# Four experts of 32 slots side by side in TensorE's array, in place of pairs of 64

## The reference

```python
g = jnp.argmax(g_logits, axis=-1)                 # one of 4 groups
top_v, top_e = lax.top_k(e_logits, 2)             # two of its 8 experts
weight = p_group * jax.nn.softmax(top_v, axis=-1)
# the 512 (token, expert) entries are sorted by expert, and for every expert e:
hid = jax.nn.silu(xc @ w_gate[e]) * (xc @ w_up[e])    # 1024 -> 256, twice
out = hid @ w_down[e]                                  # 256 -> 1024
# each token adds its two outputs, times their weights
```

## Time and profile before

| | us |
|---|---|
| median of 3 runs | 2312.27 (2310.9 to 2316.02) |
| the profiled execution | 2313.08, its span 2311.3 |
| weights of the experts start to load | 216.5 |
| first and last expert matmul | 253.3, 488.8 |
| PE busy over the span | 1864.6 (81%) |

### The profile page before, as it was taken

How to read it: one execution, slowest core, us unless ns; L and a number is a source line. 1 busy time by engine, 2 the same in 40 slices (tenths; PEclk the granted TensorE clock), 3 DMA queues, 4 the chain that set the end, 5 groups by cost and what they waited for, 6 DMA issues and landing times. The chain is left out here.

```text
span 2311.3 us, 20289 instructions
## 1 busy us (share of the span) xinstructions
PE 1864.6 (81%) x6462; PEld 993.5 (43%) x6462; DVE 1307.9 (57%) x3163; ACT 612.0 (26%) x1396; POOL 741.8 (32%) x707
## 2 busy tenths in 40 slices
PE   5887899959877988786778788988789787776877
PEld 3556322329555444332333336756444433332333
DVE  4455300037277556667676646545756666667664
ACT  3353111123622222222222214543222222222221
POOL 1000154310103443453534420330443344453542
PEclk9998899979988899898988998998899999898999
DMA  8843999967548999999999977543999999999997
GB/s 291 318 165 143 375 400 399 401 207 232 208 160 314 409 410 409 421 422 421 421 422 410 422 321 248 183 163 102 342 409 409 412 421 422 421 421 421 413 422 293
DMA packets 211846, 786.03 MB, mean 340 GB/s; under 512 B 29243, under 2 KB 89403, under 8 KB 145948
## 3 DMA queue, kind: packets, MB, share of 16 engines
q0 software_dynamic: 85408, 547.20, 57.7%
q1 hardware_dynamic: 126332, 237.53, 28.5%
HBM read 806.56 MB, written 13.98 MB: 355 GB/s over the span
## 5 line engine op out<-in xcount | busy, mean ns | idle before, releaser
L1845 PE MATMUL psum<-peer_rows,peer_diag 128*128 128x512 f32 x2048 | 978.3, 638 | 271.0 <-ACT peer_diag L1901 270.9
L1938 POOL DMA_INDIRECT peer_rows<-in_peer_uv,peer_expert x512 | 580.0, 1133 | 882.1 <-PE psum L1845 673.6
L2017 DVE CUSTOM_DVE_ANT_0 peer_rows<-peer_rows,peer_norm_h 128x1024 f32<-128x1024 f32 x512 | 620.0, 1224 | 429.3 <-DMA peer_rows<-in_peer_uv,peer_expert 429.2
L1845 PEld LDWEIGHTS psum<-peer_rows,peer_diag 128*128 128x128 f32 x2048 | 412.3, 205 | 821.0 <-issue 502.6
L1901 ACT ACTIVATE peer_diag<-ident,peer_weight 128x128 f32<-128x128 f32 x512 | 164.8, 390 | 739.3 <-DVE peer_weight L2027 703.7
L1217 PE MATMUL psum<-moe_ring,moe_W 128*64 128x512 f32 x640 | 145.4, 600 | 16.2 <-DMA moe_ring<-in_moe_w,moe_piece_i 9.7
L1824 PE MATMUL psum<-peer_norm_hT,peer_q_raw 128*128 128x256 f32 x512 | 118.4, 387 | 9.8 <-DMA peer_q_raw<-in_peer_q 6.6
L1824 PEld LDWEIGHTS psum<-peer_norm_hT,peer_q_raw 128*128 128x128 f32 x512 | 98.2, 194 | 33.8 <-DMA peer_q_raw<-in_peer_q 11.4
L1293 POOL COPY moe_W<-moe_X 128x512 f32 x40 | 24.3, 620 | 252.5 <-issue 196.7
L1217 PEld LDWEIGHTS psum<-moe_ring,moe_W 128*64 128x64 f32 x640 | 46.8, 138 | 111.3 <-issue 111.1
L1894 ACT ACTIVATE peer_dots<-peer_dots 128x4 f32<-128x4 f32 (+1 forms) x140 | 28.5, 204 | 248.4 <-DVE peer_dots L2017 248.2
(11 more groups left out here) (425 smaller groups left out, 2245.0 us busy)
## 6 DMA issues: line engine op xcount, KB each, us to landing
moe_ring<-in_moe_w SPq DMA_DIRECT2D x192, 512.0 KB
mix_mod_w<-in_mod_w SPq DMA_DIRECT2D x32, 768.0 KB, 7.1
peer_q_raw<-in_peer_q SPq DMA_DIRECT2D x32, 512.0 KB
fox_w_raw<-in_fox_in SPq DMA_DIRECT2D x32, 512.0 KB
mix_w_raw<-in_w_in SPq DMA_DIRECT2D x24, 512.0 KB
lru_mod_w<-in_mod_w SPq DMA_DIRECT2D x16, 768.0 KB
fox_mod_w<-in_mod_w SPq DMA_DIRECT2D x16, 768.0 KB, 6.8
lru_in_raw<-in_lru_in SPq DMA_DIRECT2D x22, 512.0 KB
```

What stands on the lines that cost most here:

```text
L1845: ins = pe.matmul(Y(t, c), diag[:, j % 2, k, :], R[:, place_of(m), D + c * BANK:D + (c + 1) * BANK], start=m % PICKS == 0, stop=m % PICKS ...
L1938: pool.indirect_dma_start(R[:, place_of(m), :], None, uv, bass.IndirectOffsetOnAxis(ap=expert[:, t, at:at + 1], axis=0))\
L2017: dve.tensor_tensor_reduce(here, here, norm.h[:, t, :], 1.0, 0.0, ALU.mult, ALU.add, dots[:, t, at:at + 1]).then_inc(dotted, 1)
```

## The change

A group is now four subs of 32 slots (`BY = 4`, `SUB = 32`). The experts make eight own groups. Four overflow groups follow own groups 2, 3, 5 and 6: they hold 16 subs, for experts with more than 32 tokens (each up to 8 subs in all). Four experts use 32 columns each of the array. The ring keeps its 30 places, and a group now has 24 pieces. POOL makes four cuts a group, and 24 requests an overflow group. The table on which partition belongs to which sub is made by comparisons with multiples of 32 (`block_of`), and the tables of overflow subs have 16 rows in place of 8.

```diff
-    SUB = P // 2
-    OVER = 8
-    EXTRA = 3
+    BY = 4
+    SUB = P // BY
+    OVER = 16
+    EXTRA = 7
     SUBS = EXPERTS + OVER
-    PAIRS = SUBS // 2
+    QUADS = SUBS // BY
...
-    order = []
-    for p in range(EXPERTS // 2):
-        order.append(p)
-        if p % 3 == 0 and 0 < p < 13:
-            order.append(EXPERTS // 2 + p // 3 - 1)
-    is_extra = lambda x: order[x] >= EXPERTS // 2
+    own = EXPERTS // BY
+    order = [0, 1, 2, own, 3, own + 1, 4, 5, own + 2, 6, own + 3, 7]
+    is_extra = lambda x: order[x] >= own
...
-            turn += [(x, j, a) for j in range(GP) for a in range(2)]
+            turn += [(x, j, a) for j in range(GP) for a in range(BY)]
...
-                    sp.dma_start(ring[:, q % LAND, :], d["moe_w"][(2 * order[x] + a) * PIECES + j]).then_inc(landed[q % LAND], 16)
+                    sp.dma_start(ring[:, q % LAND, :], d["moe_w"][(BY * order[x] + a) * PIECES + j]).then_inc(landed[q % LAND], 16)
...
                 def gate_up(x):
-                    pe.wait_ge(cut, 2 * x + 2)
+                    pe.wait_ge(cut, BY * x + BY)
                     wait_past(pe, hid_done, x)
                     for j in range(GP):
-                        pair = [number_of[x, j, a] for a in range(2)]
-                        for q in pair:
+                        four = [number_of[x, j, a] for a in range(BY)]
+                        for q in four:
                             here(q)
                         for b in range(2):
                             k = 2 * j + b
-                            for a, q in enumerate(pair):
+                            for a, q in enumerate(four):
...
                 def cut_tokens(x):
                     if x >= 2:
                         pool.wait_ge(w_used, end_of["up", x - 2])
-                    for a in range(2):
-                        n = 2 * order[x] + a
+                    for a in range(BY):
+                        n = BY * order[x] + a
...
-                            for a in range(2):
+                            for a in range(BY):
                                 load_extra(x + 1, j, a)
...
-                upper, lower, row = (half[:, n:n + 1] for n in range(3))
-                TS(upper, here[:, 0:1], float(SUB), ALU.is_ge)
-                TS(lower, upper, -1.0, ALU.mult, 1.0, ALU.add)
-                chain.step(dve.scalar_tensor_tensor(row, upper, -float(SUB), here[:, 0:1], ALU.mult, ALU.add))
+                passed, row = block_of[:, 0:BY + 1], block_of[:, BY + 1:BY + 2]
+                TS(passed, number[:, 0:BY + 1], float(SUB), ALU.mult)
+                TS(passed, passed, here[:, 0:1], ALU.is_le)
+                chain.step(dve.tensor_reduce(row, block_of[:, 1:BY + 1], AX, ALU.add))
+                chain.step(dve.scalar_tensor_tensor(row, row, -float(SUB), here[:, 0:1], ALU.mult, ALU.add))
+                TT(block_of[:, 0:BY], block_of[:, 0:BY], block_of[:, 1:BY + 1], ALU.subtract)
...
-                by_pair = rows[:, 0, :].rearrange("p (n a) -> p n a", a=2)
-                TS(rows[:, 1, 0:PAIRS], by_pair[:, :, 0], lower, ALU.mult)
-                chain.step(dve.scalar_tensor_tensor(rows[:, 1, 0:PAIRS], by_pair[:, :, 1], upper, rows[:, 1, 0:PAIRS], ALU.mult, ALU.add))
-                chain.step(dve.tensor_copy(rows_i[:, :], rows[:, 1, 0:PAIRS]))
+                by_four = rows[:, 0, :].rearrange("p (n a) -> p n a", a=BY)
+                TT(by_four, by_four, spread(block_of[:, 0:BY], 1, QUADS), ALU.mult)
+                RED(rows[:, 1, 0:QUADS], by_four, ALU.add)
+                chain.step(dve.tensor_copy(rows_i[:, :], rows[:, 1, 0:QUADS]))
```

More of the change, by code:

```diff
@@ L1116, in stage_moe @@
         about = sb("about", [P, 4, OVER])
-        half = sb("half", [P, 3])
-        begin, rows, rows_i = sb("begin", [P, 2, SUBS]), sb("rows", [P, 4, SUBS]), sb("rows_i", [P, PAIRS], U32)
+        block_of = sb("block_of", [P, BY + 3])
+        begin, rows, rows_i = sb("begin", [P, 2, SUBS]), sb("rows", [P, 4, SUBS]), sb("rows_i", [P, QUADS], U32)
         start_i, piece_f, piece_i = sb("start_i", [P, SUBS], U32), sb("piece_f", [P, OVER, PIECES]), sb("piece_i", [P, OVER, PIECES], U32)
@@ L1167, in load_down @@
                         for j in range(GP, PIECES):
-                            for a in range(2):
+                            for a in range(BY):
                                 load(x, j, a)
                 load_up(0)
-                for x in range(1, PAIRS):
+                for x in range(1, QUADS):
                     load_up(x)
                     load_down(x - 1)
-                load_down(PAIRS - 1)
+                load_down(QUADS - 1)
             @block.tensor
@@ L1222, in down @@
                 def down(x, j):
-                    pair = [number_of[x, GP + j, a] for a in range(2)]
+                    four = [number_of[x, GP + j, a] for a in range(BY)]
                     if j == 0:
@@ L1245, in _ @@
                 pe.wait_ge(x_dve, KD // 2)
-                for x in range(PAIRS):
+                for x in range(QUADS):
                     gate_up(x)
@@ L1253, in _ @@
                 for j in range(HJ):
-                    down(PAIRS - 1, j)
-                pe.wait_ge(hid_done, PAIRS)
-                pe.wait_ge(hidT_ready, PAIRS)
+                    down(QUADS - 1, j)
+                pe.wait_ge(hid_done, QUADS)
+                pe.wait_ge(hidT_ready, QUADS)
             @block.scalar
@@ L1269, in _ @@
                     act.activation(X[:, k, :], XB(k), ACT.Copy, scale=norm.cols[:, k:k + 1]).then_inc(x_act, 1)
-                for x in range(PAIRS + 2):
+                for x in range(QUADS + 2):
                     if x >= 2:
@@ L1295, in load_extra @@
                 def load_extra(x, j, a):
[L1296 removed]
+                    q, o = number_of[x, j, a], BY * order[x] + a - EXPERTS
                     pool.wait_ge(w_used, q - LAND + 1)
@@ L1305, in _ @@
                 cut_tokens(0)
-                for x in range(PAIRS + 2):
+                for x in range(QUADS + 2):
                     if x == 2:
                         pool.wait_ge(tables, 1)
-                    if x + 1 < PAIRS:
+                    if x + 1 < QUADS:
                         cut_tokens(x + 1)
@@ L1316, in _ @@
                             .then_inc(sent[x % 2], 16)
-                    if x + 1 < PAIRS and is_extra(x + 1):
+                    if x + 1 < QUADS and is_extra(x + 1):
                         for j in range(GP):
-                            for a in range(2):
+                            for a in range(BY):
                                 load_extra(x + 1, j, a)
-                    if x < PAIRS and is_extra(x):
+                    if x < QUADS and is_extra(x):
                         for j in range(GP, PIECES):
-                            for a in range(2):
+                            for a in range(BY):
                                 load_extra(x, j, a)
                 for k in range(2):
-                    pool.wait_ge(sent[k], 16 * len(range(k, PAIRS, 2)))
+                    pool.wait_ge(sent[k], 16 * len(range(k, QUADS, 2)))
                 pool.wait_ge(w_used, len(turn))
```

10 lines of the change are left out of this document (5 added, 5 removed).

## The result

| | before | after |
|---|---|---|
| median of 20 runs each, us | 2312.70 (2304.18 to 2321.22) | 2319.22 (2313.69 to 2327.9) |
| the profiled execution's span | 2311.3 | 2325.7 |
| first expert matmul starts, last one ends | 253.3, 488.8 | 257.7, 494.6 |
| weights start to load, last ones land | 216.5, 483.7 | 217.1, 492.0 |
| DVE ends the MoE, next stage starts | 504.8, 507.7 | 510.8, 515.5 |

The ratio is 1.0031, 95% interval 1.002 to 1.0041: the change makes the kernel slower by 0.3%, 7.2 us. The profiled executions stand 14 us apart. 7.7 of that have come about when the next stage starts; the other 7 arise in stages that the change doesn't touch, in one execution each, and I leave them out.

What follows compares the result with a forecast made beforehand. The prediction took matmuls and weight transfers as nearly balanced before, transfers as the bound after. Its terms, - 4.9 + 2.0 + 3.1 + 2.4 - 2.4 = + 0.2 us, gave a median of 2312.5 us, range 2306 to 2321.

Steps and rivals of the forecast that it cites:

- (a): Likeliest case, chance 0.55: expert weight transfers bound before and after, terms nearly cancel, 2312.5 us, own range 2308 to 2317.
- rival (c): Own groups: TensorE at half clock lengthens holes, start gap and end; + 5.7 us, so 2318; chance 0.15.
- The main reading: Expert stage: TensorE and weight transfers balanced to within a per cent before; 86 us less matmul work gains nothing beyond transfers.
- Step 1: Expert matmuls: four 32-column tiles run side by side, 10.82 us a group, so TensorE has 86 us less to do.
- Step 2: Ring holes of the kernel before close, as TensorE frees places as soon as pieces land: -4.9 us.
- Step 3: Start of the experts: first matmul moves from 253.3 to 255.1, leaving a transfer gap of + 2.0 us (1 to 3.5).
- Step 4: Overflow requests that move nothing: 40 more requests and scatters at 0.078 us each, + 3.1 us in transfers.
- Step 5: Ring, where one own group lies between two overflow groups: two new holes of 1.2 us, + 2.4 (0 to 6).
- Step 6: POOL's overflow requests: issued far enough ahead, 3 us in hand, so 0 us added.
- rival (d): Overflow groups: POOL's requests come late, 2 x 7 us, about 2326; chance 0.08.
- Step 7: End of the experts: only one down step after the last piece, 2.6 us in place of 5, - 2.4.
- The clock: TensorE in own groups: waits for DMA let the clock drop; at 1.2 GHz the sum would be some 5 us higher.

Runs made afterwards that it cites:

- e2: The kernel after with its eight own groups alone, the four overflow groups left out: 2305.23 us, ratio 0.9965 to the kernel before.
- e3: The kernel before with its sixteen own pairs alone, the four overflow pairs left out: 2303.84 us, ratio 0.9951 to the kernel before.
- e1: The kernel after with two own groups between any two overflow groups, the last overflow group at the very end: 2331.53 us, ratio 1.008 to the kernel before.
- e4: The kernel after without its 96 overflow requests; ring numbers, places and matmuls of overflow groups stay: 2312.73 us, ratio 0.9989 to the kernel before.
- e8: The kernel before without its 48 overflow requests; numbers and matmuls of overflow pairs stay: 2303.77 us, ratio 0.9959 to the kernel before.
- e6: The kernel after with two own groups between first and second overflow group, and POOL waiting for overflow tables one group earlier: 2317.06 us, ratio 1.0014.
- e7: The kernel after with 26 places in the ring in place of 30: 2330.99 us, ratio 1.0085 to the kernel before.
- e9: The kernel after with 33 places in the ring, room taken from tiles idle in the MoE: 2310.76 us, ratio 0.9993 to the kernel before.
- f3: The kernel after with two unused matmuls before each gate_up step of own groups from the third on: 2319.6 us, ratio 1.0024 to the kernel before.

## Why the prediction was right and wrong

The time lies in the predicted range, but not in its likeliest case: no change had the largest chance, 0.55, and it is slower by 0.31%. The median is 6.7 us above the figure given and 2 above the end of (a)'s own range. That the range holds it is owed to the room left for rival (c), and this is in part luck: (c)'s size is right, and its mechanism, half clock at the holes, did happen, but it accounts for the smaller part of them.

**The main reading** (transfers bound before and after, so 86 us less of TensorE buy nothing) is shown by e2 and e3. It even held more strongly than I read it. I took the pairs for balanced between matmuls and transfers to a per cent, and without overflow they wait 37.8 us for weights.

**Step 1**, matmuls: right at full clock, 7.07 us for 64, 1.92 for 16. TensorE's busy time fell by 56.5 us and not by 86, as many bursts ran at 1.2 GHz (L1215 has a mean of 728 ns for its 592).

**Step 2**, the hole of before closes: right, 260 GB/s became 410.

**Step 3**, the later start: mis-sized, 5.4 us of gap in place of 2.0. The first expert matmul was 4.4 us later and not 1.8. Two more cuts cost as expected (PE starts 2.9 us behind POOL's first copy, 1.7 before). But 1.75 us are the 32 routing matmuls ahead of it, which took 7.04 us in this execution and 5.29 before. The change doesn't touch these; the clock was lower. Counted from where the weights start to load, the first matmul comes on average 2.1 us later with four (after, e1, e2, e4) than with pairs (before, e3), so the start itself was about right. The gap was still too small in the forecast: in the seven profiles of groups of four with overflow or without and 30 places, this stretch loses 2.6 to 5.4 us, 4.0 on average.

**Step 4**, requests, + 3.1: wrong as a difference. The price in transfers is roughly there: after loses 4.5 us more than e4 outside the holes, 0.047 for each of 96 where I had 0.078. Of the rest of the 9.7, 2.6 lie at the boundary (4.7 against 2.0); what remains is within the uncertainty. For the pairs the same count, before against e8 from 286 to 455, gives 3.7 us, 0.076 for each of 48: the price per request that I had, but for half as many it is nearly as large a sum, so the difference is 0.9 us in transfers and not 3.1. In all, the cost is as large for the pairs with 48 (9.5) as for the fours with 96 (9.7), within some 5 us, where I took it as proportional to their number.

**Step 5**, two new holes, + 2.4: this is the step that failed. The places and the mechanism were right: one own group between two overflow groups, and e6, e7 and e9 close one and resize them. The size was 4.8 and 5.7 us, about 1 of each the requests' lower rate, so 4 to 5 each in place of 1.2. I had reckoned as if 16 DMA engines moved piece by piece and all six pieces (7.7 us) had to be gone before anything was lost. In 2-us bins the rate fell from 388 to 222 GB/s at 340. What I should have used stood in rows 4: at the end of the kernel before, the transfers did not stop but thinned out, down to 85 GB/s by 480 to 484. Here the rate falls while the last pieces are still under way. That this is the main reason was only argued. Another part is in the traces: my 1.8 us for the step before the refill was 1.9 at the first hole and 3.4 at the second, at 1.2 GHz, which I had only in the upper bound; f3 took it away and 1.7 us of loss with it. Why the holes with a full-clock step still lose 4 to 5 us stays open.

**Step 6**, POOL at 0: right as a cost, wrong as a statement that the requests are there in time. All 8.8 us of TensorE's waits for them (9.7 before, in twelve small ones) lie in the second and the fourth overflow group, 4.5 and 4.3 us (360.46 above is the longest), where rival (d) had 7 each. They cost little: transfers run on at 395 and 394 GB/s meanwhile, and TensorE's next own pieces keep it waiting again, for 3.0 us at 374.20 and 3.5 at 477.22.

**Step 7**, the end, - 2.4: right, 494.6 - 492.0 = 2.6 us in place of 5. What I said came behind it "stays as it is" was wrong by 1.7 us, at the boundary of the stage. No term stood for it.

Set against the profile, step 3 lacks 3.4 us, step 5 some 6.1 and the boundary 1.7, and step 4 has 2.2 too much in transfers: + 0.2 becomes + 9.2, where the next stage starts 7.7 later. The sum explains the result to 1.5 us, with step 5 as its largest error.

The four kernels with and without overflow divide the result in another way. Without overflow, four against pairs is + 0.0014. The reserved numbers cost 0.0024 with four (e4 less e2) and 0.0008 with pairs (e8 less e3): + 0.0016. The requests cost 0.0042 and 0.0041: + 0.0001. Together 0.0031, that is 3.2, 3.7 and 0.2 us, each with 4 to 6 us of uncertainty by the intervals. So none of the three is clear of nothing by its time; that holes are the largest part rests on the profiles.

**The clock.** The Trainium skill (TensorE: Matmul & The Clock Gate, section HAM oscillation) says that waits for DMA let the clock fall. The trace agrees in the main, with 0.85 in place of 0.99 and bursts of 3.4 us, though not after every wait (433.47). The price that I worked out by it, some 5 us, was too high: f3_warm gave most of the clock back, and with it 1.7 us at the second hole and, by the ratios, 1.6 us in all, which isn't clear of nothing.

## What to carry to other kernels

Before you speed up matmuls in a stage with a DMA share near 1, run it with less work around it (e3 here): if its engine then waits for data, the faster layout can't pay. Where a ring's numbers include places that nothing is loaded into, count what is still under way when they fill the ring, and take more loss than an even drain gives (here 4 to 5 us in place of 1.2). Look also at which step frees the first places behind such a hole, and at the clock that it runs at. Grouping four in place of two doubles such runs of numbers; the ring has to grow with them.

## What was not expected of the hardware

- A request that moves nothing isn't cheap: 96 of them, 137 small packets each (15264 packets of that queue from 253 to 490, less 474 rows, over 108 requests and scatters), took 9.7 us, and 48 took 9.5, each within some 4 us.
- The boundary behind the MoE took 1.6 to 2.0 us with no requests for up pieces, 2.9 and 3.1 with 32 of them, 4.4 to 4.7 with 64, in all 14 profiles. Whose work that is, and why requests for down pieces leave it alone, stays open.
- A granted clock of 0.80 to 0.86 over most of 200 us cost little: TensorE waited 61.5 us for own pieces beside it. It showed only where a burst at 1.2 GHz stood between the transfers and their next free places, 3.42 us in place of 1.92.
